# Six orders for the three products of a weight chunk, one for each loop job of each phase, and one small tensor less

## The chip, the core and the metric

The kernel runs on one core of one Trainium2 chip. The metric is the device time of one execution in microseconds (us). One execution of the kernel before was recorded by the hardware profiler; all rows below are read from it.

## The reference

Two decoder layers over 256 tokens of width 2048, all in float32. Layer 0 mixes tokens with an RWKV-7 recurrence, layer 1 with block attention over one block of keys and values; after each mixer and each FFN stands a layer norm over `ALPHA * h + branch`.

```python
mixed = _rwkv7_time_mix(h, ...)  if layer < N_A_LAYERS  else  _moba_attention(h, b_w_q[j], b_w_o[j], k_pad, v_pad, k_mean)
h = _layernorm(ALPHA * h + mixed, ln1_w[layer], ln1_b[layer])
h = _layernorm(ALPHA * h + _swiglu(h, ffn_w_gate[layer], ffn_w_up[layer], ffn_w_down[layer]),
               ln2_w[layer], ln2_b[layer])
# _swiglu: (jax.nn.silu(x @ w_gate) * (x @ w_up)) @ w_down
```

Nearly all of the arithmetic is products of the 256 tokens with weight matrices: eight of 2048x2048 (k, r, v, o, kv_k, kv_v, q and ao in the kernel's names), and for each layer gate and up (2048x5632) and down (5632x2048).

## The kernel before

A weight matrix is taken in **jobs** of 512 columns, and a job in **chunks** of 2x128 rows (KC = 2), 128x1024 numbers in SBUF. A job of 2048 rows has 8 chunks, one of the down projection 22. For each chunk SyncE loads `raw[:, s]` (512 KB), ScalarE writes the rounded high half `whi[:, s]` (line 951), VectorE writes the rest `wlo[:, s] = raw - whi` (lines 1237 and 1510), with s one of four slots (RING = 4). The activations are split too: `ahi` and `alo` (hidden ones of the FFN: `hThi` and `hTlo`).

TensorE then makes three products for a chunk, for each of its two blocks of 128 rows (k2) and each of the two halves of the tokens (t): high activations by high weights (HIHI), high by low (HILO) and low by high (LOHI). The activations are the stationary tile (128x128, loaded by an LDWEIGHTS before every matmul) and the weights are the moving tile (128x512). So a chunk has 12 matmuls. They add up in two PSUM banks, `ps[:, 2 * parity + t]`, one for each half of the tokens; parity is that of the job. In the kernel before, the order is k2, then t, then HIHI, HILO, LOHI (lines 495 to 497):

```python
pe.wait_ge(split_done, c + (ch + 1))
...
        mm(o, hi[:, k, tok], whi[:, s, k2, :], start=(k == 0), stop=False)
        mm(o, hi[:, k, tok], wlo[:, s, k2, :], start=False, stop=False)
        last = mm(o, lo[:, k, tok], whi[:, s, k2, :], start=False, stop=(k == kt - 1))
last.then_inc(chunk_used, 1)
```

The semaphore `split_done` says that both halves of a chunk are there; `chunk_used` gives the slot back to ScalarE. `job` waits for the two banks and runs its chunks. Pairs of jobs, one of each parity, stand in hardware loops: `jobs` for the projections of layer 0 (`proj`, three times one pair), the down projections (one pair of 22 chunks each), K, V and Q (`kvq`, five pairs) and the attention output (`ao`, one pair), and `ffn` for gate and up (10 pairs in each layer, with 8 transposes of the hidden tile between the jobs, line 881). The jobs before and after the loops (`first_job`, `normed_job`, `last_job`) are written out; `last_job` finishes one half of the tokens ahead of the other over its last four chunks (lines 520 to 522), so that it runs 24 matmuls into one bank.

The layer norm of a half of the tokens is VectorE's `last_block`: mean and variance, then a reciprocal square root in three Newton steps on tensors of 128x1 (lines 1544 to 1552). It uses `half_var`, a tensor of 128x2 numbers, for minus half of the variance. `small` is a tensor of 128x32 of which columns 0 and 1 are used.

Of the kernel before, what the change touches and what calls it, by code (L numbers as in the profile page):

```python
# [29 lines left out]
P = 128  # L30
D = 2048
T = 256
TT = T // P
KT = D // P
NB = 512
NJ = D // NB
FF = 5632
FT = FF // P
FB = FF // NB
KC = 2  # L40
RING = 4
PLAIN = 3
CJ = KT // KC
CF = FT // KC
LR = 96
LG = 256
HD = 64
# [47 lines left out]
PH = {}  # L95
_c = _j = 0
for _name, _jobs, _per in (("proj", 12, CJ), ("wo", NJ, CJ), ("up0", 2 * FB, CJ), ("down0", NJ, CF), ("kvq", 12, CJ),
                           ("ao", NJ, CJ), ("up1", 2 * FB, CJ), ("down1", NJ, CF)):
    assert _c % RING == 0 and _j % 2 == 0
# [30 lines left out]
def trunk(nc, x, rows, rwkv_rows, lora, w, consts, ln_rows, y):  # L130
    with ExitStack() as ctx:
# [3 lines left out]
        def sb(name, shape, dt=F32, stack=ctx):  # L135
            return stack.enter_context(nc.sbuf_tensor(name, shape, dt))
# [5 lines left out]
        whi = sb("whi", [P, RING, KC, NB], F32R)  # L142
        wlo = sb("wlo", [P, RING, KC, NB], F32R)
# [5 lines left out]
        var = sb("var", [P, TT])  # L149
        rstd = sb("rstd", [P, TT])  # L150
        small = sb("small", [P, 32])
        half_var = sb("half_var", [P, TT])
        gsm = sb("gsm", [P, 5, 8])
        nsmall = sb("nsmall", [P, 48])
        idle = sb("idle", [P, 10])
# [3 lines left out]
        ahi = sb("ahi", [P, KT, T], F32R)  # L159
        alo = sb("alo", [P, KT, T], F32R)  # L160
# [4 lines left out]
        hThi = sb("hThi", [P, FT, T], F32R)  # L165
        hTlo = sb("hTlo", [P, FT, T], F32R)
        ps = ctx.enter_context(nc.psum_tensor("ps", [P, 8, NB], F32))
# [316 lines left out]
        def _(pe):  # L484
            mm, tr = nc.tensor.matmul, nc.tensor.transpose

            def chunk(c, ch, parity, kt, hi, lo):

                s = (ch + (CF * parity if kt == FT else 0)) % RING
                pe.wait_ge(split_done, c + (ch + 1))  # L490
                for k2 in range(KC):
                    k = ch * KC + k2
                    for t in range(TT):
                        o, tok = ps[:, 2 * parity + t, :], slice(t * P, (t + 1) * P)
                        mm(o, hi[:, k, tok], whi[:, s, k2, :], start=(k == 0), stop=False)  # L495
                        mm(o, hi[:, k, tok], wlo[:, s, k2, :], start=False, stop=False)  # L496
                        last = mm(o, lo[:, k, tok], whi[:, s, k2, :], start=False, stop=(k == kt - 1))  # L497
                last.then_inc(chunk_used, 1)

            def job(c, u, parity, kt, hi, lo):  # L500

                pe.wait_ge(bank_free[parity], u + 1)
                for ch in range(kt // KC):
                    chunk(c, ch, parity, kt, hi, lo)

            def last_job(c, u, kt, hi, lo):

# [43 lines left out]
                    if src is not None and ch + 4 < CJ:  # L551
                        transposes(ch + 4)

            def jobs(c0, j0, n, kt, hi, lo):

                per = kt // KC
                with pe.Fori(0, n // 2) as i:
                    for b in range(2):
                        job(i * (2 * per) + (c0 + b * per), i + j0 // 2, b, kt, hi, lo)


            pe.wait_ge(id_in, 16)
            for g in range(KT // KC):
# [3 lines left out]
                for k2 in range(KC):  # L567
                    for t in range(TT):
                        k = g * KC + k2
                        last = tr(ps[:, 4 + g % 4, k2 * T + t * P:k2 * T + (t + 1) * P], xn[:, t, k * P:(k + 1) * P], ident[:])  # L570
# [7 lines left out]
            for n, (m, buf) in enumerate(((w1, L_), (a1, A_))):  # L578
                mx = buf.rearrange("p t (k n) -> p (t k) n", n=T)
                for k in range(KT):  # L580
                    pe.wait_ge(lmix_done, n * KT + k + 1)
                    last = mm(ps[0:LR, 4 + n, 0:T], m[:, k, :], mx[:, k, :], start=(k == 0), stop=(k == KT - 1))  # L582
# [3 lines left out]
            for k in range(KT):  # L586
                pe.wait_ge(lmix_done, 2 * KT + k + 1)
                for m in range(2):
                    last = mm(ps[:, 6 + m, 0:T], g1[:, k, m * P:(m + 1) * P], mx[:, k, :], start=(k == 0), stop=(k == KT - 1))  # L589
# [5 lines left out]
            for n in range(2 * NJ):  # L595
                if n >= 2:
                    pe.wait_ge(lora2_copied, n - 1)
                h, m = ((hw, w2), (ha, a2))[n // NJ]
                for t in range(TT):
                    last = mm(ps[:, 4 + 2 * (n % 2) + t, :], h[0:LR + 1, t * P:(t + 1) * P],  # L600
                              m[0:LR + 1, (n % NJ) * NB:(n % NJ + 1) * NB], start=True, stop=True)
                last.then_inc(lora2_made, 1)

            for n in range(3):
                c, j = n * NJ * CJ, n * NJ
                first_job(c, j // 2, act_ready, n * (KT // KC))
                job(c + CJ, j // 2, 1, KT, ahi, alo)
                jobs(c + 2 * CJ, j + 2, NJ - 2, KT, ahi, alo)
            for b in range(2):
                pe.wait_ge(bank_free[b], 7)  # L610

# [208 lines left out]
            for n in range(NJ):  # L820
                for t in range(TT):
                    for k in range(2):
                        last = mm(ps[:, 2 * n + t, :], hg[:, k, t * P:(t + 1) * P], g2[:, k, n * NB:(n + 1) * NB], start=(k == 0), stop=(k == 1))
                last.then_inc(gate_made, 1)

            c, j = PH["wo"]
# [45 lines left out]
            def ffn(layer):  # L872
                c0, j0 = PH[f"up{layer}"]
                u0 = layer * FB

                def h_transposes(i):

                    pe.wait_ge(bank_free[1], i + (j0 // 2 + 2 - u0))
                    for f in range(4):
                        for t in range(TT):  # L880
                            last = tr(ps[:, 4 + f // 2, (f % 2) * T + t * P:(f % 2) * T + (t + 1) * P], gtmp[:, t, f * P:(f + 1) * P], ident[:])  # L881
                    last.then_inc(h_tr, 1)

                normed_job(2 * layer, f"up{layer}")
                with pe.Fori(0, FB - 1) as i:
                    job(i * (2 * CJ) + (c0 + 2 * CJ), i + (j0 // 2 + 1), 0, KT, ahi, alo)
                    h_transposes(i + u0)
                    job(i * (2 * CJ) + (c0 + 3 * CJ), i + (j0 // 2 + 1), 1, KT, ahi, alo)
                    pe.wait_ge(hlo_done, i + (u0 + 1))
                h_transposes(u0 + FB - 1)  # L890
                pe.wait_ge(hlo_done, u0 + FB)
                c, j = PH[f"down{layer}"]
                jobs(c, j, NJ - 2, FT, hThi, hTlo)
                last_two(c + 2 * CF, j + 2, FT, hThi, hTlo)

            ffn(0)
            normed_job(1, "kvq")
            jobs(PH["kvq"][0] + 2 * CJ, PH["kvq"][1] + 2, 10, KT, ahi, alo)

            for b in range(2):  # L900
                pe.wait_ge(bank_free[b], PH["ao"][1] // 2 + 1)
# [1 line left out]
            with pe.Fori(0, HEADS // 4) as i:  # L903
                one = i + 1
                lane = [(al[s], 4 * s, stg[s], QKT[s], Sm[s], PT[s]) for s in range(2)]
                for q, b, st, qkt, sm, pt in lane:
                    pe.wait_ge(q["qk_staged"], one)
                    for h in range(2):
                        for n in range(4):
                            last = tr(ps[:, b + h, n * P:(n + 1) * P], st[:, n // 2, n % 2, h * P:(h + 1) * P], ident[:])  # L910
                    last.then_inc(q["qk_tr"], 1)
                for q, b, st, qkt, sm, pt in lane:
                    pe.wait_ge(q["qkt_set"], one)
                    for h in range(2):
                        mm(ps[:, b + 2 + h, 0:P], qkt[:, h, 0:P], qkt[:, h, 2 * P:3 * P], start=True, stop=True)
                        last = mm(ps[:, b + 2 + h, P:3 * P], qkt[:, h, P:2 * P], qkt[:, h, 2 * P:4 * P], start=True, stop=True)
                    last.then_inc(q["s_made"], 1)
                for q, b, st, qkt, sm, pt in lane:
                    pe.wait_ge(q["p_normed"], one)
                    for h in range(2):  # L920
                        for n in range(3):
                            last = tr(ps[:, b + h, n * P:(n + 1) * P], sm[:, h, n * P:(n + 1) * P], ident[:])
                    last.then_inc(q["pt_made"], 1)
                for q, b, st, qkt, sm, pt in lane:
                    pe.wait_ge(q["pt_set"], one)
                    pe.wait_ge(q["v_staged"], one)
                    for h in range(2):
                        v = st[:, 2, :, h * P:(h + 1) * P]
                        mm(ps[:, b + 2 + h, 0:T], v[:, 0], pt[:, h, 0:2 * P], start=True, stop=False, skip_group_check=True)
                        last = mm(ps[:, b + 2 + h, P:T], v[:, 1], pt[:, h, 2 * P:3 * P], start=False, stop=True, skip_group_check=True)  # L930
# [1 line left out]
            for q in al:  # L932
                pe.wait_ge(q["olo_set"], HEADS // 4)
            c, j = PH["ao"]
            jobs(c, j, NJ - 2, KT, ahi, alo)
            last_two(c + 2 * CJ, j + 2, KT, ahi, alo)
            ffn(1)

# [266 lines left out]
        def _(dve):  # L1205
# [37 lines left out]
            for g in range(KT // KC):  # L1243
                dve.wait_ge(xt_copied, g + 1)
                k = slice(g * KC, (g + 1) * KC)
# [247 lines left out]
            for n in range(NJ):  # L1493
                dve.wait_ge(gate_made, n + 1)
                c = slice(n * NB, (n + 1) * NB)
# [27 lines left out]
            def last_block(c0, kt, n, t):  # L1523

                c_next = c0 + NJ * kt // KC
                cs = slice((NJ - 1) * NB, NJ * NB)
                if t == 0:
                    dve.wait_ge(tile_done, n + 1)
                else:
                    dve.wait_ge(chunk_used, c_next)  # L1530
                ins = V.scalar_tensor_tensor(out=Zn[:, t, cs], in0=H[:, t, cs], scalar=ALPHA, in1=ps[:, 2 + t, :], op0=ALU.mult, op1=ALU.add)
                if t == 0 and c_next == CHUNKS:
                    then(ins)
                elif t == 0:
                    ins.then_inc(split_done, 1)
                    dve.wait_ge(split_done, c_next + 1)
                else:
                    ins.then_inc(bank_free[1], 1)
                    dve.wait_ge(bank_free[1], (c_jobs[n] + NJ - 1) // 2 + 2)
                then(V.bn_stats(stats[:, t, NJ - 1, :], Zn[:, t, cs]))  # L1540
                then(V.bn_aggr(mv[:, t, :], stats[:, t]))
                I32 = mybir.dt.int32
                x, hx, y0, q = (m[:, t:t + 1] for m in (var, half_var, rstd, small))
                ins = V.tensor_scalar(hx, mv[:, t, 1:2], LN_EPS, -0.5, ALU.add, ALU.mult)
                if c_next < CHUNKS:
                    ins.then_inc(split_done, 1)
                then(V.tensor_scalar(x, mv[:, t, 1:2], LN_EPS, None, ALU.add))
                then(V.tensor_scalar(q.bitcast(I32), x.bitcast(I32), 1, None, ALU.logical_shift_right))
                then(V.tensor_scalar(y0.bitcast(I32), q.bitcast(I32), -1.0, float(0x5F3759DF), ALU.mult, ALU.add))
                for _ in range(3):  # L1550
                    then(V.tensor_scalar(q, y0, y0, hx, ALU.mult, ALU.mult))
                    then(V.scalar_tensor_tensor(out=y0, in0=q, scalar=1.5, in1=y0, op0=ALU.add, op1=ALU.mult))
# [157 lines left out]
```

## Time and profile before

| | |
|---|---|
| median of the runs | 2715.93 us (two of three runs; the third was 13648.72 us) |
| the profiled execution | 2719.42 us, span 2717.6 us |
| TensorE busy | 2549.3 us, 94% |
| VectorE busy | 1445.9 us, 53% |
| ScalarE busy | 1084.7 us, 40% |
| mean granted clock of TensorE | 0.97 |
| matmuls, weight loads | 15342 each |
| read from HBM | 436.96 MB, 162 GB/s |

The median is the figure to compare. The span reaches from the first to the last instruction of the profiled execution; 1.8 us lie around it. A matmul's row gives the start as it was recorded and an end that is modelled, so that neighbouring rows overlap; the distance of starts is the measure of its pace.

### The profile page before, as it was taken

Reading aid. Unit: us, or ns where it says so; the run is one execution under the profiler, and the core shown is the slowest. Engines: PE = TensorE matmul, PEld = TensorE weight load, DVE = VectorE, ACT = ScalarE, POOL = GpSimd, SP = SyncE. Lnnn points to the kernel's source line nnn. Section 1 sums busy time; section 2 is a strip of 40 time slices with the busy share of each in tenths; the row PEclk is TensorE's granted clock in tenths of the full one; section 3 lists DMA queues with packets and bytes.
Section 4 is the critical chain, followed back from the end, with each engine's and each line's share of the span. In section 5 each row is a group of like instructions: output and inputs, shape, how many; then the busy total and the mean of one; then the engine's idle time right before and its main releaser. Section 6 shows DMA issues by size and latency. Waiting matters only on the chain.

```text
span 2717.6 us, 39424 instructions
## 1 busy us (share of the span) xinstructions
PE 2549.3 (94%) x15342; PEld 2042.7 (75%) x15342; DVE 1445.9 (53%) x1738; ACT 1084.7 (40%) x1326; POOL 139.3 (5%) x187
## 2 busy tenths in 40 slices
PE   7999968878999999999999999969999999999997
PEld 5777757766788888887887788857788888877886
DVE  4555976674654444444445644454754444444445
ACT  3444434433443434343333444443434343443332
POOL 1000014430000000000000000010000000000000
PEclk9999979889999999999999999989999999999999
DMA  5555700144466666665665666614566666666664
GB/s 173 166 170 168 214 21 8 15 137 149 147 199 186 180 185 184 185 179 161 186 187 183 199 190 187 185 54 147 150 196 185 182 185 184 185 179 193 186 187 131
DMA packets 219155, 440.75 MB, mean 162 GB/s; under 512 B 13216, under 2 KB 13248, under 8 KB 217824
## 3 DMA queue, kind: packets, MB, share of 16 engines
q1 hardware_dynamic: 214400, 413.19, 50.5%
q0 software_dynamic: 4640, 25.92, 3.4%
q8 instruction: 85, 1.39, 0.2%
q14 instruction: 30, 0.25, 0.0%
HBM read 436.96 MB, written 2.10 MB: 162 GB/s over the span
## 4 chain that ended last, share of the span: by engine, by line
PE 86%; DVE 9%; issue 2%; ACT 2%; DMA 1%; POOL 1%; DVEq 0%; ACTq 0%; SPq 0%; POOLq 0%
PE ps L495 25%; PE ps L496 25%; PE ps L497 25%; DVE wlo L1237 2%; PE ps L881 1%; PE ps L685 1%; PE ps L695 1%; PE ps L705 1%; PE ps L582 1%; PE ps L853 1%; DVE rec L1377 1%; DMA big<-lora_a 1%; DVE alo L1564 1%; PE ps L600 1%; PE ps L589 1%
## 5 line engine op out<-in xcount | busy, mean ns | idle before, releaser
L951 ACT CAST whi<-raw 128x1024 fp32r<-128x1024 f32 x772 | 807.6, 1049 | 1271.6 <-PE ps L497 1192.6
L1237 DVE TENSOR_TENSOR wlo<-raw,whi 128x1024 fp32r<-128x1024 f32 x551 | 672.1, 1225 | 700.5 <-ACT whi L951 700.0
L495 PE MATMUL ps<-whi,ahi 128*128 128x512 f32 x2364 | 940.7, 398 | 29.7 <-DVE wlo L1237 12.9
L496 PE MATMUL ps<-wlo,ahi 128*128 128x512 f32 x2364 | 935.5, 396 | 0.0
L497 PE MATMUL ps<-whi,alo 128*128 128x512 f32 x2364 | 935.2, 396 | 0.0
L495 PEld LDWEIGHTS ps<-whi,ahi 128*128 128x128 f32 x2364 | 444.3, 188 | 145.9 <-issue 37.0
L497 PEld LDWEIGHTS ps<-whi,alo 128*128 128x128 f32 x2364 | 444.1, 188 | 108.7
L496 PEld LDWEIGHTS ps<-wlo,ahi 128*128 128x128 f32 x2364 | 444.5, 188 | 107.2 <-issue 0.7
L1510 DVE TENSOR_TENSOR wlo<-raw,whi 128x1024 fp32r<-128x1024 f32 x224 | 274.0, 1224 | 332.7 <-ACT whi L951 332.5
L495 PE MATMUL ps<-whi,hThi 128*128 128x512 f32 x672 | 267.6, 398 | 5.1 <-DVE hTlo L1614 5.1
L496 PE MATMUL ps<-wlo,hThi 128*128 128x512 f32 x672 | 267.3, 398 | 0.0
L497 PE MATMUL ps<-whi,hTlo 128*128 128x512 f32 x672 | 267.1, 397 | 0.0
L495 PEld LDWEIGHTS ps<-whi,hThi 128*128 128x128 f32 x672 | 127.2, 189 | 37.0 <-issue 5.9
L496 PEld LDWEIGHTS ps<-wlo,hThi 128*128 128x128 f32 x672 | 127.1, 189 | 31.3
L497 PEld LDWEIGHTS ps<-whi,hTlo 128*128 128x128 f32 x672 | 127.1, 189 | 31.1
L1127 ACT ACTIVATE a2t<-ps,lnT 128x128 f32<-128x128 f32 x96 | 34.2, 496 | 34.1 <-PE ps L843 34.1
L1377 DVE TENSOR_TENSOR rec<-ps,big 128x512 f32<-128x512 f32 x40 | 27.6, 690 | 35.4 <-PE ps L685 34.8
L450 POOL DMA_DIRECT2D big<-ln_rows x3 | 1.7, 572 | 871.6 <-PE ps L522 851.1
L1251 DVE SCALAR_TENSOR_TENSOR big<-big,mixT 128x256 f32<-128x256 f32 x96 | 40.0, 479 | 1.5 <-PE ps L582 0.8
L1383 DVE STREAM_TRANSPOSE rec<-ps 128x512 f32<-128x512 f32 x32 | 22.8, 713 | 32.7 <-PE ps L695 32.4
L1614 DVE TENSOR_TENSOR hTlo<-ps,hThi 128x1024 f32 (+1 forms) x22 | 26.9, 1224 | 21.1 <-ACT hThi L1146 21.1
L695 PE MATMUL ps<-big,rec 64*64 64x64 f32 x960 | 32.2, 233 | 4.1 <-DVE rec L1377 3.9
(286 smaller groups left out, 1681.7 us busy)
## 6 DMA issues: line engine op xcount, KB each, us to landing
raw<-w_gate SPq DMA_DIRECT2D x176, 512.0 KB, 3.7
raw<-w_up SPq DMA_DIRECT2D x176, 512.0 KB, 3.7
raw<-w_down SPq DMA_DIRECT2D x176, 512.0 KB, 3.7
raw<-w_k SPq DMA_DIRECT2D x32, 512.0 KB, 4.2
raw<-w_r SPq DMA_DIRECT2D x32, 512.0 KB, 3.7
raw<-w_v SPq DMA_DIRECT2D x32, 512.0 KB, 4.4
raw<-w_o SPq DMA_DIRECT2D x32, 512.0 KB, 4.3
raw<-kv_k SPq DMA_DIRECT2D x32, 512.0 KB, 4.2
```

The costliest lines, as they stand in the source:

```text
L495: mm(o, hi[:, k, tok], whi[:, s, k2, :], start=(k == 0), stop=False)
L496: mm(o, hi[:, k, tok], wlo[:, s, k2, :], start=False, stop=False)
L497: last = mm(o, lo[:, k, tok], whi[:, s, k2, :], start=False, stop=(k == kt - 1))
L582: last = mm(ps[0:LR, 4 + n, 0:T], m[:, k, :], mx[:, k, :], start=(k == 0), stop=(k == KT - 1))
L589: last = mm(ps[:, 6 + m, 0:T], g1[:, k, m * P:(m + 1) * P], mx[:, k, :], start=(k == 0), stop=(k == KT - 1))
L695: quarters(lambda j, h, t, a, u, v: mm(ps[u, 2 + a, half(j)], Z[v, a, half(j)], XS[v, half(j)] if a else XT[g % 2][v, 0, half(j)], start=T ...
L951: nc.scalar.copy(whi[:, s], raw[:, s]).then_inc(hi_done, 1)
L1127: ins = A(hF[:, k, t * P:(t + 1) * P], ps[:, 4 + b, k2 * P:(k2 + 1) * P], ACT.Identity, scale=lnT[:, (n * 2) * KT + k:(n * 2) * KT + k + 1 ...
L1237: V.tensor_tensor(wlo[:, s], raw[:, s], whi[:, s].bitcast(F32), ALU.subtract).then_inc(split_done, 1)
L1251: return V.scalar_tensor_tensor(out=out, in0=xxT[:, k], scalar=mixT[:, m * KT + k:m * KT + k + 1], in1=xT[:, k, 1:T + 1], op0=ALU.mult, op ...
L1377: V.tensor_tensor(Z.rearrange("p l (j c) -> p l j c", c=CHUNK), ps[:, 0:2, 0:4 * CHUNK].rearrange("p l (j c) -> p l j c", c=CHUNK), mask_l ...
L1510: V.tensor_tensor(wlo[:, s], raw[:, s], whi[:, s].bitcast(F32), ALU.subtract).then_inc(split_done, 1)
```

## The change

A table of six orders is added, and `chunk` walks through one of them. The flags `start` and `stop` go to the first and the last matmul of each token half in the job. The matmuls, their weight loads, the wait at the chunk's first and the semaphore at its last instruction are as many as before. The loops name an order for each of their two jobs: (1, 3), (2, 4) and (5, 0) for the three projections, (2, 4) and (5, 1) for the FFN of layers 0 and 1, (1, 3) and (4, 5) for their down projections, (1, 3) for K, V and Q and (3, 0) for the attention output. All jobs outside of the loops keep order 0, which is the old one. `half_var` is gone; columns 2 and 3 of `small` take its place, and the tensors that were allocated behind it start 32 bytes lower in SBUF (`ahi` from 67936 to 67904).

```diff
+HIHI, HILO, LOHI = range(3)
+ORDERS = (
+    [(k2, t, p) for k2 in range(KC) for t in range(TT) for p in (HIHI, HILO, LOHI)],
+    [(k2, t, p) for k2 in range(KC) for p in (HIHI, HILO, LOHI) for t in range(TT)],
+    [(k2, t, p) for k2 in range(KC) for t in range(TT) for p in (HILO, HIHI, LOHI)],
+    [(k2, t, p) for k2 in range(KC) for t, p in ((0, HIHI), (0, LOHI), (1, HIHI), (1, LOHI), (0, HILO), (1, HILO))],
+    [(k2, t, p) for p in (HIHI, HILO, LOHI) for t in range(TT) for k2 in range(KC)],
+    [(k2, t, p) for k2 in range(KC) for t in range(TT) for p in (HIHI, LOHI, HILO)],
+)
...
-        half_var = sb("half_var", [P, TT])
...
-            def chunk(c, ch, parity, kt, hi, lo):
+            def chunk(c, ch, parity, kt, hi, lo, order=0):
...
                 pe.wait_ge(split_done, c + (ch + 1))
-                for k2 in range(KC):
+                for at, (k2, t, p) in enumerate(ORDERS[order]):
                     k = ch * KC + k2
...
+                    a, m = ((hi, whi), (hi, wlo), (lo, whi))[p]
+                    first = ch == 0 and t not in [x[1] for x in ORDERS[order][:at]]
+                    final = ch == kt // KC - 1 and t not in [x[1] for x in ORDERS[order][at + 1:]]
+                    last = mm(ps[:, 2 * parity + t, :], a[:, k, t * P:(t + 1) * P], m[:, s, k2, :], start=first, stop=final)
                 last.then_inc(chunk_used, 1)
...
-                jobs(c + 2 * CJ, j + 2, NJ - 2, KT, ahi, alo)
+                jobs(c + 2 * CJ, j + 2, NJ - 2, KT, ahi, alo, ((1, 3), (2, 4), (5, 0))[n])
...
-                    job(i * (2 * CJ) + (c0 + 2 * CJ), i + (j0 // 2 + 1), 0, KT, ahi, alo)
+                    job(i * (2 * CJ) + (c0 + 2 * CJ), i + (j0 // 2 + 1), 0, KT, ahi, alo, (2, 5)[layer])
                     h_transposes(i + u0)
-                    job(i * (2 * CJ) + (c0 + 3 * CJ), i + (j0 // 2 + 1), 1, KT, ahi, alo)
+                    job(i * (2 * CJ) + (c0 + 3 * CJ), i + (j0 // 2 + 1), 1, KT, ahi, alo, (4, 1)[layer])
...
-                x, hx, y0, q = (m[:, t:t + 1] for m in (var, half_var, rstd, small))
+                x, hx, y0, q = (m[:, t:t + 1] for m in (var, small[:, TT:2 * TT], rstd, small))
```

TensorE, in the FFN loop of layer 0, where the second job begins after the transposes. Before (names are out<-moving,stationary):

```order
L881 MATMUL ps<-ident,common 128x128 x8
L490 REGISTER_ALU
L495 MATMUL ps<-whi,ahi 128x512
L496 MATMUL ps<-wlo,ahi 128x512
L497 MATMUL ps<-whi,alo 128x512
L495 MATMUL ps<-whi,ahi 128x512
```

and with the change, in which this job has order 4:

```order
L888 MATMUL ps<-ident,common 128x128 x8
L498 REGISTER_ALU
L504 MATMUL ps<-whi,ahi 128x512 x4
L504 MATMUL ps<-wlo,ahi 128x512 x4
L504 MATMUL ps<-whi,alo 128x512 x4
```

The 12 matmuls of the chunk stand in three groups of four instead of four groups of three. In the first job of the same loop, order 2, the rows of a chunk read with the change:

```order
L498 ISA
L504 MATMUL ps<-wlo,ahi 128x512
L504 MATMUL ps<-whi,ahi 128x512
L504 MATMUL ps<-whi,alo 128x512
L504 MATMUL ps<-wlo,ahi 128x512
```

The product with the low half stands first, and after the two with the high half comes the next token half. On VectorE the rows of a token half's layer norm (after `last_block`'s sum) were

```order
L1541 BN_AGGR mv<-stats 128x2
L1544 TENSOR_SCALAR half_var<-mv 128x1
L1547 TENSOR_SCALAR var<-mv 128x1
L1548 TENSOR_SCALAR small<-var 128x1
L1549 TENSOR_SCALAR rstd<-small 128x1
L1551 TENSOR_SCALAR small<-rstd,half_var 128x1
```

and with the change

```order
L1548 BN_AGGR mv<-stats 128x2
L1551 TENSOR_SCALAR small<-mv 128x1
L1554 TENSOR_SCALAR var<-mv 128x1
L1555 TENSOR_SCALAR small<-var 128x1
L1556 TENSOR_SCALAR rstd<-small 128x1
L1558 TENSOR_SCALAR small<-rstd,small 128x1
```

Nothing has moved there; one operand's tensor is another.

## Rows read from the trace of the kernel before

**Rows 1.** The page: span and busy time by engine

```profile
span 2717.6 us, 39424 instructions
...
PE 2549.3 (94%) x15342; PEld 2042.7 (75%) x15342; DVE 1445.9 (53%) x1738; ACT 1084.7 (40%) x1326; POOL 139.3 (5%) x187
```

**Rows 2.** The page: the chain that ended last, shares of the span by line

```profile
PE ps L495 25%; PE ps L496 25%; PE ps L497 25%; DVE wlo L1237 2%; PE ps L881 1%; PE ps L685 1%; PE ps L695 1%; PE ps L705 1%; PE ps L582 1%; PE ps L853 1%; DVE rec L1377 1%; DMA big<-lora_a 1%; DVE alo L1564 1%; PE ps L600 1%; PE ps L589 1%
```

**Rows 3.** Timeline of TensorE: start us, duration us, engine, line, op

```profile
703.27 0.40 PE L495 MATMUL ps<-whi,ahi 128*128 128x512 f32 x1
703.51 0.39 PE L496 MATMUL ps<-wlo,ahi 128*128 128x512 f32 x1
703.74 0.40 PE L497 MATMUL ps<-whi,alo 128*128 128x512 f32 x1
...
704.44 0.39 PE L497 MATMUL ps<-whi,alo 128*128 128x512 f32 x1
704.67 0.40 PE L495 MATMUL ps<-whi,ahi 128*128 128x512 f32 x1
...
708.87 0.40 PE L495 MATMUL ps<-whi,ahi 128*128 128x512 f32 x1
...
709.58 0.39 PE L520 MATMUL ps<-whi,ahi 128*128 128x512 f32 x1
...
715.17 0.39 PE L520 MATMUL ps<-whi,ahi 128*128 128x512 f32 x1
```

**Rows 4.** Windows: stretch, length, busy us of each engine, clock, DMA share

```profile
800.00:1200.00 400.00, 400.00 (x1750) 322.36 (x1749) 192.84 (x159) 162.41 (x158) 0.00 (x0) 1.00 0.64 184
1200.00:1300.00 100.00, 93.92 (x397) 75.17 (x396) 41.88 (x35) 36.15 (x35) 0.00 (x0) 0.95 0.55 165
```

**Rows 5.** Timeline of all engines inside the FFN loop of layer 0

```profile
1199.10 1.23 DVE L1237 TENSOR_TENSOR wlo<-raw,whi 128x1024 fp32r<-128x1024 f32 x1 [1.57 <-ACT whi L951]
...
1200.62 0.40 PE L495 MATMUL ps<-whi,ahi 128*128 128x512 f32 x1
1200.62 0.19 PEld L496 LDWEIGHTS ps<-wlo,ahi 128*128 128x128 f32 x1
1200.82 1.05 ACT L951 CAST whi<-raw 128x1024 fp32r<-128x1024 f32 x1 [1.75 <-PE ps L497]
1200.85 0.39 PE L496 MATMUL ps<-wlo,ahi 128*128 128x512 f32 x1
```

**Rows 6.** Waits of TensorE: who waited for whom, us in total, times, longest

```profile
PE ps L495 <- DVE wlo L1237: 12.9, 13, 3.0
```

**Rows 7.** Groups of weight loads by line: count, busy us, mean ns

```profile
L496 PEld LDWEIGHTS ps<-wlo,ahi 128*128 128x128 f32 x2364 | 444.5, 188 | 107.2 <-issue 0.7
...
L497 PEld LDWEIGHTS ps<-whi,alo 128*128 128x128 f32 x2364 | 444.1, 188 | 108.7
```

**Rows 8.** Operations on small tensors: count, duration ns min/median/max

```profile
L1551 DVE TENSOR_SCALAR small<-rstd,half_var x24: 272/273/275, 717.7 to 2708.5; 128x1 f32<-128x1 f32 x24
L1544 DVE TENSOR_SCALAR half_var<-mv x8: 153/154/156, 717.1 to 2706.8; 128x1 f32<-128x1 f32 x8
...
L1552 DVE SCALAR_TENSOR_TENSOR rstd<-small,rstd x24: 158/159/161, 718.1 to 2708.8; 128x1 f32<-128x1 f32 x24
...
L1549 DVE TENSOR_SCALAR rstd<-small x8: 153/153/154, 717.6 to 2707.3; 128x1 int32<-128x1 int32 x8
```

**Rows 9.** Lines 644 and 1251: count, duration ns min/median/max, starts

```profile
L644 PEld LDWEIGHTS ps<-ident,rec x24: 140/230/230, 373.1 to 528.7; 128*128 128x128 f32 x24
L644 PEld LDWEIGHTS ps<-ident,a2t x24: 139/143/230, 395.5 to 555.7; 128*128 128x128 f32 x24
...
L1251 DVE SCALAR_TENSOR_TENSOR big<-big,mixT x96: 469/479/487, 17.9 to 267.8; 128x256 f32<-128x256 f32 x96
```

**Rows 10.** Timeline of TensorE after the pause at 159 us

```profile
164.05 0.77 PE L495 MATMUL ps<-whi,ahi 128*128 128x512 f32 x1 [4.63 <-issue]
...
165.04 0.63 PE L497 MATMUL ps<-whi,alo 128*128 128x512 f32 x1
165.47 0.63 PE L495 MATMUL ps<-whi,ahi 128*128 128x512 f32 x1
```

More of the change, by code:

```diff
@@ L485, in _, with job @@
             mm, tr = nc.tensor.matmul, nc.tensor.transpose
-            def chunk(c, ch, parity, kt, hi, lo):
+            def chunk(c, ch, parity, kt, hi, lo, order=0):
                 s = (ch + (CF * parity if kt == FT else 0)) % RING
                 pe.wait_ge(split_done, c + (ch + 1))
-                for k2 in range(KC):
+                for at, (k2, t, p) in enumerate(ORDERS[order]):
                     k = ch * KC + k2
[L493 to L497, printed above, removed]
+                    a, m = ((hi, whi), (hi, wlo), (lo, whi))[p]
+                    first = ch == 0 and t not in [x[1] for x in ORDERS[order][:at]]
+                    final = ch == kt // KC - 1 and t not in [x[1] for x in ORDERS[order][at + 1:]]
+                    last = mm(ps[:, 2 * parity + t, :], a[:, k, t * P:(t + 1) * P], m[:, s, k2, :], start=first, stop=final)
                 last.then_inc(chunk_used, 1)
-            def job(c, u, parity, kt, hi, lo):
+            def job(c, u, parity, kt, hi, lo, order=0):
                 pe.wait_ge(bank_free[parity], u + 1)
                 for ch in range(kt // KC):
-                    chunk(c, ch, parity, kt, hi, lo)
+                    chunk(c, ch, parity, kt, hi, lo, order)
             def last_job(c, u, kt, hi, lo):
@@ L552, in first_job, with jobs @@
                         transposes(ch + 4)
-            def jobs(c0, j0, n, kt, hi, lo):
+            def jobs(c0, j0, n, kt, hi, lo, orders):
                 per = kt // KC
@@ L558, in jobs @@
                     for b in range(2):
-                        job(i * (2 * per) + (c0 + b * per), i + j0 // 2, b, kt, hi, lo)
+                        job(i * (2 * per) + (c0 + b * per), i + j0 // 2, b, kt, hi, lo, orders[b])
             pe.wait_ge(id_in, 16)
@@ L892, in ffn @@
                 c, j = PH[f"down{layer}"]
-                jobs(c, j, NJ - 2, FT, hThi, hTlo)
+                jobs(c, j, NJ - 2, FT, hThi, hTlo, ((1, 3), (4, 5))[layer])
                 last_two(c + 2 * CF, j + 2, FT, hThi, hTlo)
@@ L897, in _ @@
             normed_job(1, "kvq")
-            jobs(PH["kvq"][0] + 2 * CJ, PH["kvq"][1] + 2, 10, KT, ahi, alo)
+            jobs(PH["kvq"][0] + 2 * CJ, PH["kvq"][1] + 2, 10, KT, ahi, alo, (1, 3))
             for b in range(2):
@@ L934, in _ @@
             c, j = PH["ao"]
-            jobs(c, j, NJ - 2, KT, ahi, alo)
+            jobs(c, j, NJ - 2, KT, ahi, alo, (3, 0))
             last_two(c + 2 * CJ, j + 2, KT, ahi, alo)
```

## The prediction

> **What bounds the kernel now.** I first read the head of the page. TensorE is busy for 2549.3 of 2717.6 us, VectorE for 53% and ScalarE for 40% of the span [rows 1]. Of the chain that ended last, three quarters are the lines 495 to 497 on TensorE, the three products of a weight chunk; the largest share of another engine is 2% [rows 2]. TensorE is therefore the bound. What matters for an edit that only reorders those three lines is the pitch: the time from the start of one matmul to the start of the next. A row's own duration of 396 ns overlaps its neighbour and says nothing of it.
>
> The timeline of TensorE gives the pitch. Eight groups of three, 24 matmuls, start from 703.27 to 708.87 us: 5.60 us, so 233.3 ns each [rows 3]. A chunk has 12 of them, 2.80 us. In a stretch of 400 us inside a loop TensorE has no idle time and the granted clock is 1.00 [rows 4]. 512 columns at 2.4 GHz, which is what a granted clock of 1.00 stands for, are 213.3 ns, so 20.0 ns of each pitch are something else.
>
> Supply is not the limit. ScalarE makes the high half of a chunk in 1.05 us and then stands for 1.75 us until TensorE gives a slot back; VectorE makes the low half in 1.23 us and stands for 1.57 us [rows 5]. The chain of a refill is 1.05 + 1.23 us plus hand-over, under 2.5 us, from the end of chunk n to the readiness of chunk n+4, which is wanted three chunks or 8.4 us later. In the whole run TensorE waits at line 495 for a low half only 12.9 us in 13 places [rows 6].
>
> **The change, part by part.** The loops named in the diff run 552 chunks: 48 in the three projections, 160 in each FFN, 44 in each down projection, 80 for K, V and Q and 16 for the attention output. Order 0 keeps 16 of them (the second job of the third projection and of the attention output). So 536 chunks, 6432 matmuls, are reordered; at 233.3 ns they are 1500.8 us, 55% of the span. By orders: 150 chunks run order 1, 88 order 2, 78 order 3, 110 order 4, 110 order 5.
>
> What is not changed: a chunk still has 12 matmuls with 12 weight loads; its first instruction still waits for the low half of the whole chunk, and its last still hands the slot back. So no wait moves relative to the chunk, even where an order begins with the low half (order 2), and nothing is queued behind a new wait. All six orders begin with a stationary tile of the high activations, as before. Per engine the instruction counts are equal, so the loops' code is as long as before.
>
> What is changed is the neighbourhood of each matmul. Each transition can keep or change the PSUM bank, the stationary tile and the moving tile. I counted them over the 552 chunks, chunk borders included.
>
> (a) Bank changes: 4 a chunk before; 12, 4, 8, 6 and 4 in orders 1 to 5. In sum 2208 before, 3940 after, 1732 more. The trace has both kinds: from 709.58 us the last job runs 24 matmuls into one bank, and its 24th start after that is 715.17 us: 5.59 us, against 5.60 us for the 24 in which 8 change the bank [rows 3]. Two readings to 0.01 us can be off by 0.02 us together, over 8 changes 2.5 ns each. I take zero; the bound is 1732 x 2.5 ns = 4.3 us either way.
>
> (b) Repeated stationary tiles: 4 a chunk before (line 495 to 496), kept only by orders 0 and 2; 2208 before, 416 after, 1792 fewer. If a repeated tile were cheaper, 495 to 496 would be the short step. It is 0.24 us at one place, where the next one is 0.23 [rows 3], and 0.23 us at another [rows 5]. The load of line 496, which repeats the tile, takes a mean of 188 ns over the run, as that of 497 does [rows 7]. The repeat is loaded again and costs the same. I take zero; with 5 ns of reading error the bound is 1792 x 5 = 9.0 us either way.
>
> (c) One neighbourhood is new: same bank, new stationary tile, same moving tile (high-high, then low-high for the same tokens). Orders 2, 3 and 5 have 4 a chunk: 276 x 4 = 1104. No row of before shows it. Its two nearest rows differ in one thing each: 496 to 497 (same bank, both tiles new) is 0.23 us, 497 to 495 from one token half to the other (new bank, same moving tile; 704.44 to 704.67 us) 0.23 us [rows 3]. I take the same 233.3 ns. Downward it can't go below the columns: -20.0 ns x 1104 = -22.1 us. Upward the far bound is a weight load that comes out from under the running matmul, which is a rival below.
>
> (d) The half-variance moves into columns 2 and 3 of another small tensor. Two operations use it: 24 of 273 ns at line 1551 read it, 8 of 154 ns at line 1544 write it [rows 8]. These stand on the path between the last product and the next phase. After the change line 1551 reads and writes one tensor, at different columns. The nearest row is line 1549, which reads that small tensor and takes 153 ns, where line 1544, which reads and writes elsewhere, takes 154 [rows 8]. I take zero. If 1551 fell to line 1552's 159 ns it would give 24 x 0.114 = 2.7 us; if all 32 doubled they would cost 24 x 0.273 + 8 x 0.154 = 7.8 us.
>
> (e) The tensors behind it start 32 bytes lower, among them both activation halves. Weight loads of 128x128 from rec, ahead of it, and from a2t, behind it, show minima of 140 and 139 ns [rows 9], though their starts differ by 32 bytes modulo 64. VectorE's line 1251 reads rows that start 4 bytes further each time and stays within 469 to 487 ns over 96 runs [rows 9]. Zero.
>
> The sum: 2719.42 us of the profiled execution (span 2717.6 and 1.8 around it) + 0 = 2719.4 us. That execution is 3.5 us or 0.13% over the median of the runs, 2715.93 us, so the forecast is the median, **2716 us**.
>
> **Rivals.** First, slower: in the new neighbourhood (c) the weight load is no longer taken ahead. Now a load starts with the matmul before the one that it serves, as at 1200.62 us, and is done after 0.19 us, 0.04 us before it is wanted [rows 5]. If the moving tile held back the load in these 1104 places, each would show up to 187 ns: 206 us, 2922 us. It decides (2%, 54.3 us) from 49 ns per place, or 290 fully exposed loads. Against it: the step 497 to 495 keeps the moving tile too, and hides its load [rows 3].
>
> Second, faster: the 20.0 ns over the columns are a price of the old order, for instance of three products in a row into one bank, and all reordered matmuls lose it: 6432 x 20.0 ns = 128.6 us, 2587 us. The supply could follow: the chunk would be 2.56 us against 1.23 us of VectorE work. Against it: the pitch is the same within one bank and over changes of it. The Trainium skill (TensorE: Matmul & The Clock Gate, "Wait — 56ns, not 53.3ns?") measured 215.7 ns for 512 columns with bf16, 17.6 ns under the 233.3 ns here; by that figure the same rival would be an estimated 113 us, 2603 us. The trace does not agree with the figure at any transition.
>
> Third, the phase of the clock. After a pause of 4.63 us, at 159 us, the next starts are 0.43 us apart, the 1.2 GHz level, where they are 0.23 us apart otherwise [rows 3, 10]. The 100 us from 1200 us have such a stretch too and a mean clock of 0.95 [rows 4]: 5% of full speed missing over 100 us is 5 us lost. None of the pauses is touched, but one more such stretch would cost about that, one less would give it back. That stays inside "no change".
>
> That the change does nothing at all is the forecast itself; that it is not carried out is excluded by the rows of the order.
>
> **How the numbers follow.** No change to speak of: 0.94. Load exposed: 0.03, ends slower. The 20 ns lost: 0.03, ends faster. The low end takes (c) down to its floor, 2716 - 22 = 2694 us. The high end takes (a) and (b) at their bounds, 2716 + 13.3 = 2729, with a little of the clock 2730 us. Between them lies more than 8 in 10; I don't narrow it, since these are the bounds of what no row excludes. Faster or slower by over 2%, which is about what a measurement of this kernel can tell, has 0.03 each, within 2% 0.94.
>
> **What would show it.** In the changed kernel's timeline the 12 starts of a chunk in orders 1 to 5 must span 2.80 us; a load after "high-high, low-high" must still start with the matmul before; the window from 800 to 1200 us must be 400 us busy at 1.00 with as many matmuls; line 1551's successor must stay at 273 ns. Wrong would be: steps of unequal length within a chunk, a weight load that begins after its neighbour's start, or idle time at the chunk's first matmul.

## The result and the profile after

The changed kernel takes 2681.2 us (median of four runs, 2677.46 to 2682.99), the kernel before 2715.93 us. The ratio of the runs is 0.9871, with a 95% interval of 0.9852 to 0.989. It is faster by 34.7 us, 1.3%. The forecast was 2716 us with a range of 2694 to 2730 us; the result lies 13 us under its low end.

The page of the changed kernel: span and busy time, chain by line, and the groups of the products (as in [rows 1], [rows 2] and [rows 7]; all six lines of products now have line 504):

```profile
span 2681.0 us, 39424 instructions
...
PE 2513.0 (94%) x15342; PEld 2047.2 (76%) x15342; DVE 1446.8 (54%) x1738; ACT 1086.0 (41%) x1326; POOL 138.8 (5%) x187
...
PE ps L504 74%; DVE wlo L1244 2%; PE ps L888 1%; PE ps L702 1%; PE ps L692 1%; PE ps L712 1%; PE ps L589 1%; PE ps L860 1%; DVE big L1258 1%; DVE rec L1384 1%; PE ps L607 1%; PE ps L596 1%; DVE alo L1571 1%; PE ps L529 0%; PE ps L527 0%
...
L504 PEld LDWEIGHTS ps<-whi,ahi 128*128 128x128 f32 x2364 | 445.3, 189 | 131.9 <-issue 36.7
L504 PEld LDWEIGHTS ps<-whi,alo 128*128 128x128 f32 x2364 | 446.6, 189 | 101.9
L504 PEld LDWEIGHTS ps<-wlo,ahi 128*128 128x128 f32 x2364 | 446.9, 189 | 98.9 <-issue 0.7
```

The instruction counts are the same, and the busy times of the other engines are within 1.3 us of what they were. TensorE's fell by 36.3 us, where the span lost 36.6 us. The waits of TensorE at these products did not fall. Before, they were 12.9 us for the low half [rows 6], and

```profile
PE ps L495 <- issue: 11.6, 3, 4.6
```

With the change they are

```profile
PE ps L504 <- DVE wlo L1244: 13.1, 14, 3.1
PE ps L504 <- issue: 11.6, 3, 4.6
```

So the products themselves came closer together. The windows of the changed kernel (as [rows 4]; the number in brackets behind TensorE's busy time counts its matmuls):

```profile
800.00:1200.00 400.00, 400.00 (x1786) 329.32 (x1785) 195.91 (x161) 166.95 (x161) 0.00 (x0) 1.00 0.64 188
```

At the same granted clock of 1.00 the 400 us hold 1786 matmuls, where they held 1750 [rows 4].

The telling rows are those of a place that the orders don't touch. The last job of the first output projection is written out and keeps the old order. The timeline of TensorE there, the first row and the one 24 matmuls later (before: 709.58 to 715.17 us, 5.59 us [rows 3]):

```profile
703.66 0.39 PE L527 MATMUL ps<-whi,ahi 128*128 128x512 f32 x1
...
709.16 0.39 PE L527 MATMUL ps<-whi,ahi 128*128 128x512 f32 x1
```

That is 5.50 us, 229 ns a matmul. And the two jobs that are written out ahead of the first loop, and so ahead of every reordered chunk, already have that pitch. Twelve steps of the old order in the second of them:

```profile
100.06 0.39 PE L504 MATMUL ps<-whi,ahi 128*128 128x512 f32 x1
100.29 0.39 PE L504 MATMUL ps<-wlo,ahi 128*128 128x512 f32 x1
100.52 0.39 PE L504 MATMUL ps<-whi,alo 128*128 128x512 f32 x1
...
102.80 0.40 PE L504 MATMUL ps<-whi,ahi 128*128 128x512 f32 x1
```

2.74 us, 228 to 229 ns. Meanwhile two stretches show the old pitch of 233.3 ns: the second projection of layer 0 (161.8 to 252.8 us) and K, V and Q (1496 to 1748 us), both with jobs of the old order and reordered ones in them. In the loop for K, V and Q, from the first to the second of these rows there are 24 matmuls of order 3, 5.60 us:

```profile
1600.05 0.40 PE L504 MATMUL ps<-whi,ahi 128*128 128x512 f32 x1
...
1605.65 0.40 PE L504 MATMUL ps<-whi,ahi 128*128 128x512 f32 x1
```

I took all the records of starts and cut them into groups of 12 products that follow one another without another matmul between them. Of 724 groups, 119 are at 233.3 ns and most of the others (570) at 228.9. All the products of this kind are 3 x (2364 + 672) in the loops' lines and 192 in the last jobs, 9300. (1 - 119/724) x 9300 x 4.44 ns = 34.5 us, which accounts for the gain of 34.7 us. All six orders occur at 228.9 ns, and orders 0 to 4 at 233.3 ns too. The cause was thus to be looked for in the other half of the edit: without the half-variance tensor the activation halves start at 67904, not 67936.

### The profile page after: what moved, and what is told of

It reads as the page before. It is cut to its first block, busy times and chain, and to the rows that moved or that the text cites. A ratio compares the mean times of both kernels' runs of the same rounds, so it can differ in the third digit from the quotient of the medians.

```text
span 2681.0 us, 39424 instructions
## 1 busy us (share of the span) xinstructions
PE 2513.0 (94%) x15342; PEld 2047.2 (76%) x15342; DVE 1446.8 (54%) x1738; ACT 1086.0 (41%) x1326; POOL 138.8 (5%) x187
## 4 chain that ended last, share of the span: by engine, by line
PE 85%; DVE 10%; ACT 2%; issue 2%; DMA 1%; POOL 1%; DVEq 0%; ACTq 0%; POOLq 0%
PE ps L504 74%; DVE wlo L1244 2%; PE ps L888 1%; PE ps L702 1%; PE ps L692 1%; PE ps L712 1%; PE ps L589 1%; PE ps L860 1%; DVE big L1258 1%; DVE rec L1384 1%; PE ps L607 1%; PE ps L596 1%; DVE alo L1571 1%; PE ps L529 0%; PE ps L527 0%
## 5 line engine op out<-in xcount | busy, mean ns | idle before, releaser
L504 PE MATMUL ps<-whi,ahi 128*128 128x512 f32 x2364 | 853.0, 397 | 29.7 <-DVE wlo L1244 13.1
L504 PE MATMUL ps<-whi,alo 128*128 128x512 f32 x2364 | 845.5, 393 | 0.0
L504 PE MATMUL ps<-wlo,ahi 128*128 128x512 f32 x2364 | 828.8, 394 | 0.0
L504 PE MATMUL ps<-whi,hThi 128*128 128x512 f32 x672 | 247.3, 395 | 5.1 <-DVE hTlo L1621 5.1
L504 PE MATMUL ps<-whi,hTlo 128*128 128x512 f32 x672 | 247.1, 395 | 0.0
L504 PE MATMUL ps<-wlo,hThi 128*128 128x512 f32 x672 | 239.4, 394 | 0.0
```

What stands on the lines that cost most here:

```text
L504: last = mm(ps[:, 2 * parity + t, :], a[:, k, t * P:(t + 1) * P], m[:, s, k2, :], start=first, stop=final)
```

## Experiments

Each kernel below is one of the two kernels of the case with a small edit. Theory A: the starts of the tiles in SBUF set the pitch. Theory B: the orders do. The weight halves stand ahead of the half-variance tensor in the list of tensors, at 32896, and did not move.

**The slot alone.** The kernel before, with this edit only:

```diff
-        half_var = sb("half_var", [P, TT])
...
-                x, hx, y0, q = (m[:, t:t + 1] for m in (var, half_var, rstd, small))
+                x, hx, y0, q = (m[:, t:t + 1] for m in (var, small[:, TT:2 * TT], rstd, small))
```

> The old order in every job; only the half-variance tensor is gone, so that the activation halves start 32 bytes lower (67904 in place of 67936). Theory A (the start of the activation tiles modulo 64 bytes sets the pitch): the whole gain is here, 2675 to 2685 us, pitch 228.9 ns in most stretches. Theory B (the orders bring it): 2716 us, pitch 233.3 ns everywhere.

2681.76 us, ratio 0.9857 (0.984 to 0.9874): the whole gain. This edit also changes the operand on VectorE; that it is not the cause is seen in the kernels below, where a spare tensor alone moves the pitch.

**The orders alone.** The changed kernel, with the tensor put back:

```diff
+        half_var = sb("half_var", [P, TT])
...
-                x, hx, y0, q = (m[:, t:t + 1] for m in (var, small[:, TT:2 * TT], rstd, small))
+                x, hx, y0, q = (m[:, t:t + 1] for m in (var, half_var, rstd, small))
```

> The six orders, with the half-variance tensor kept, so that every tensor starts where it did before. Theory A: 2716 us and 233.3 ns in all orders. Theory B: 2675 to 2685 us.

2716.78 us, ratio 1.0001 (0.9991 to 1.0011). The window of this kernel:

```profile
800.00:1200.00 400.00, 400.00 (x1750) 322.36 (x1749) 192.53 (x158) 162.07 (x157) 0.00 (x0) 1.00 0.63 184
```

The 400 us hold 1750 matmuls as before. Theory B has fallen: six orders, 6432 reordered matmuls, and nothing to measure.

**32 bytes higher.** The kernel before, with a spare tensor ahead of the activations, which start at 67968:

```diff
         idle = sb("idle", [P, 10])
+        spare = sb("spare", [P, 8])
```

> The old order and the half-variance tensor kept; a spare tensor of 32 bytes is put ahead of the activations, which start at 67968, a multiple of 64 and of 128. Theory A with a grain of 64 bytes: as with 32 bytes less, 2675 to 2685 us. With a grain of 128 (67904 is 64 past a multiple of 128): another time, 2716 us or something between. Theory B: 2716 us.

2653.8 us, ratio 0.9757 (0.974 to 0.9774), better than both kernels of the case. That was outside of what either theory had foreseen. The timeline of its last job, 24 matmuls apart, and its window:

```profile
701.27 0.39 PE L521 MATMUL ps<-whi,ahi 128*128 128x512 f32 x1
...
706.71 0.39 PE L521 MATMUL ps<-whi,ahi 128*128 128x512 f32 x1
```

```profile
800.00:1200.00 400.00, 400.00 (x1803) 331.93 (x1802) 197.67 (x162) 168.59 (x163) 0.00 (x0) 1.00 0.65 189
```

5.44 us, 226.7 ns, and that is the pitch in every stretch. 9300 x 6.6 ns = 61 us, nearly all of the 63 us by which it is under the kernel before (2716.92 us on the same chip).

**The weights moved instead.** The same 32 bytes ahead of both operands, so that the weights start at 32928 and the activations at 67968:

```diff
+        spare = sb("spare", [P, 8])
         with ExitStack() as early:
             rec2 = sb("rec2", [P, 8192], stack=early)
```

> The old order; the spare 32 bytes stand ahead of the weight halves, so that the moving tiles start 32 bytes past a multiple of 64 and the stationary tiles at one. If only the stationary tile's start matters: 2675 to 2685 us. If each of the two must start at a multiple of 64, or if they must start alike modulo 64: 2716 us, pitch 233.3 ns. Theory B: 2716 us.

2715.48 us, ratio 0.9994 (0.9984 to 1.0004). The activations start where they did in the kernel with 32 bytes more, but the pace is the old one. So it is not the stationary tile's start alone that counts. The distance of the two starts is 35040 here and in the kernel before. That gave theory R: only the distance counts, modulo some grain. Its rival, theory O: each operand pays for its own start.

**Both at 32.** Weights at 32928, activations at 68000: neither is a multiple of 64, and the distance is that of the kernel with 32 bytes more.

```diff
+        spare = sb("spare", [P, 8])
         with ExitStack() as early:
             rec2 = sb("rec2", [P, 8192], stack=early)
...
         idle = sb("idle", [P, 10])
+        spare2 = sb("spare2", [P, 8])
```

> The old order; spare tensors put the weight halves at 32928 and the activation halves at 68000, both 32 past a multiple of 128. Theory R (only the distance of the two operands' starts modulo 128 counts; so far 0 gave 226.7 ns, 64 mostly 228.9 and 96 233.3): distance 0, 226.7 ns, 2650 to 2660 us. Theory O (each operand must start at a multiple of 64, or pays for itself): 233.3 ns or more, 2716 us or more.

2657.13 us, ratio 0.9781 (0.9764 to 0.9797). The timeline of the last job, 24 apart:

```profile
697.56 0.39 PE L522 MATMUL ps<-whi,ahi 128*128 128x512 f32 x1
...
703.00 0.39 PE L522 MATMUL ps<-whi,ahi 128*128 128x512 f32 x1
```

5.44 us again. Theory O has fallen; the distance counts.

**The activations at 32** past a multiple of 128, the weights unmoved (a spare tensor of 16 numbers in place of 8, ahead of the activations).

> The old order; weight halves at 32896 (multiple of 128), activation halves at 68000 (32 past one). Theory R: distance 32, not measured before; equal to 96 if the sign does not count, 233.3 ns and 2716 us. Theory O: 233.3 ns, as with 96, since it is 32 past a multiple of 64.

2716.97 us in one run, 5.60 us for the 24 (707.28 to 712.88): 233.3 ns. Both theories had that, so this run tells them apart no further; it gives the pitch at distance 32.

**The weights at 64** (a spare tensor of 16 numbers ahead of the weights, and the half-variance tensor dropped).

> The old order without the half-variance tensor; weight halves at 32960 (64 past a multiple of 128), activation halves at 67968 (a multiple of 128). Theory R: distance 64, 228.9 ns in most stretches, about 2680 us. Theory O with a grain of 128 for the stationary tile alone: 226.7 ns, 2654 us.

2679.68 us in one run, 5.49 us for the 24 (703.47 to 708.96): as in the changed kernel, at other starts and the same distance, and as theory R had it; the 2654 us of the rival did not come. The stretches at 233.3 ns are not the same, though: here the second projection, most of the third (285.7 to 331.8 us) and the first gate and up jobs of layer 1 (1932 to 1983 us) are at 233.3 ns, while K, V and Q run at 228.9. In the kernel with the slot alone it is K, V and Q and those first jobs of layer 1.

**The low half of the weights alone** moved by 32 bytes; the high half and the activations start as in the kernel with 32 bytes more:

```diff
         whi = sb("whi", [P, RING, KC, NB], F32R)
+        spare = sb("spare", [P, 8])
         wlo = sb("wlo", [P, RING, KC, NB], F32R)
```

> The old order; as in the kernel with 32 bytes more (226.7 ns), but the low weight half starts 32 past a multiple of 128 while the high half stays at one. If the price is paid matmul by matmul: only the steps that begin or end at the product with the low half are longer, a mean near 229 ns, 2675 to 2685 us. If one misplaced tensor slows the whole stream: 233.3 ns, 2716 us. Theory O with the stationary tile alone: 226.7 ns.

2701.86 us in one run, between the two cases foreseen. The timeline of the down projection, three steps of a kind and the row 12 matmuls on:

```profile
1300.41 0.39 PE L496 MATMUL ps<-whi,hThi 128*128 128x512 f32 x1
1300.64 0.40 PE L497 MATMUL ps<-wlo,hThi 128*128 128x512 f32 x1
1300.88 0.39 PE L498 MATMUL ps<-whi,hTlo 128*128 128x512 f32 x1
1301.10 0.39 PE L496 MATMUL ps<-whi,hThi 128*128 128x512 f32 x1
...
1303.18 0.39 PE L496 MATMUL ps<-whi,hThi 128*128 128x512 f32 x1
```

2.77 us for 12, 231 ns. In this down projection the three steps have means of 230.8 ns (from line 496), 236.7 (from line 497, the low half's product) and 225.8 (from line 498): against 226.7 ns, the two steps that end or begin at the misplaced tile are 4.1 and 10.0 ns longer, and the third is 0.9 ns shorter. K, V and Q look the same. But in the gate and up loops, 3840 of the 9300 products, the same layout runs at the old pace. The row at the start of a group of three and the one 12 matmuls on:

```profile
1000.35 0.40 PE L496 MATMUL ps<-whi,ahi 128*128 128x512 f32 x1
...
1003.15 0.40 PE L496 MATMUL ps<-whi,ahi 128*128 128x512 f32 x1
```

2.80 us, 233.3 ns, though two of the three products have the best distance, and the window from 800 to 1200 us holds 1751 matmuls, where the kernel before has 1750. In the groups of 12 of the whole run 336 are at 233.3 ns, 223 at 231.1 and 134 at 231.7. So neither of the two cases foreseen holds alone: the price is partly paid at the misplaced product, and in other stretches it holds the whole stream at 233.3 ns. What decides between them is open.

**A wider grain.** Activations at 68096: the distance is 35200, a multiple of 128 but not of 256 (spare of 40 numbers).

> The old order; activation halves at 68096, weight halves at 32896: the distance is a multiple of 128 but, unlike in the kernel with 32 bytes more, not of 256. Theory R128 (nothing beyond 128 counts): 226.7 ns, 2650 to 2660 us. Theory R256 (the distance modulo 256 counts): a longer pitch than 226.7 ns, towards 228.9.

2704.93 us, ratio 0.9953 (0.9935 to 0.9972). The timeline of the last job, 24 apart:

```profile
708.43 0.39 PE L521 MATMUL ps<-whi,ahi 128*128 128x512 f32 x1
...
714.00 0.39 PE L521 MATMUL ps<-whi,ahi 128*128 128x512 f32 x1
```

5.57 us, 232 ns: a grain of 128 is too narrow. The pitch is longer than 226.7 ns, as theory R256 had it, but not near the 228.9 ns that it leant to.

Activations at 68224: the distance is a multiple of 512 (spare of 72 numbers).

> The old order; activation halves at 68224, so that the distance is a multiple of 512, the bytes of one stationary tile's row. Theory R128: 226.7 ns, 2650 to 2660 us. If the price goes on halving with a wider grain: under 226.7 ns, 2620 to 2640 us.

2657.38 us, ratio 0.979 (0.9773 to 0.9806), 5.44 us for the 24 (696.00 to 701.44): the same 226.7 ns as at a multiple of 256 only. The grain is 256.

**The orders where the distance is right** (spare of 16 numbers in the changed kernel, activations at 67968).

> The six orders, with activation halves at 67968 (distance a multiple of 128). The orders bring nothing by this theory: 226.7 ns in all of them, 2650 to 2660 us, as the old order at the same starts (2653.8). If orders count where the starts are right: a difference to it of over 5 us.

2658.52 us, ratio 0.9793 (0.9777 to 0.9809), 5.44 us for the 24 (699.35 to 704.79). The interval of the old order at these starts, 0.974 to 0.9774, ends just below, a gap of under 0.1%, and the 4.7 us between the two medians are inside the 5 us that the expectation allowed; the pitch is 226.7 ns with both, and the kernel with a distance of a multiple of 512, in the old order, has 2657.38 us. The orders bring nothing here either.

**Distance 96**, a spare of 32 numbers.

> The old order; activation halves at 68064, 96 past a multiple of 256 from the weight halves (32896). If the size of the distance alone counts, falling away from 32: between the 233.3 ns at 32 and the 232.4 ns at 128, 2700 to 2718 us. If an odd multiple of 32 is always the worst: 233.3 ns, 2716 us.

2726.4 us in one run. The timeline of its last job, 24 matmuls apart:

```profile
713.09 0.40 PE L521 MATMUL ps<-whi,ahi 128*128 128x512 f32 x1
...
718.72 0.40 PE L521 MATMUL ps<-whi,ahi 128*128 128x512 f32 x1
```

5.63 us, and 1747 matmuls in the window from 800 to 1200 us: the slowest of all, slower than both expectations had it.

**Distance 64**, a spare of 24 numbers.

> The old order; activation halves at 68032, 64 past a multiple of 256 from the weight halves; 192 was 228.9 ns in most stretches. If the sign of the distance does not count: 228.9 ns, 2675 to 2685 us. If it does: another pitch.

2718.77 us in one run. The window of this kernel:

```profile
800.00:1200.00 400.00, 400.00 (x1750) 321.97 (x1749) 192.76 (x158) 161.89 (x157) 0.00 (x0) 1.00 0.63 184
```

1750 matmuls as before, and 5.60 us for the 24 (708.39 to 713.99). 64 is not like 192, so the sign counts there; 32 and 224 have the same pitch.

The whole series, where "distance" is the start of the activation halves less that of the weight halves, modulo 256 (it is the same for every slot, tile and hidden half). The labels are e1 for the slot alone, e2 for the orders alone, and so on: e3 32 bytes higher, e4 the weights moved, e5 both at 32, e6 the activations at 32, e7 the wider grain, e8 the weights at 64, e10 the multiple of 512, e11 the orders at the right distance, e12 distance 96, e13 distance 64. The kernel before took 2716.9 to 2717.5 us in the rounds of these runs; e6, e8, e12 and e13 are single runs. The low half alone (e9) is left out, since its two weight halves have different distances, 0 and 224.

| distance | kernel | starts (weights, activations) | 24 matmuls of the last job | time |
|---|---|---|---|---|
| 0 | e3, e5, e10, e11 | 32896, 67968; 32928, 68000; 32896, 68224; 32896, 67968 | 5.44 us each | 2653.8, 2657.1, 2657.4, 2658.5 us |
| 32 | e6 | 32896, 68000 | 5.60 us | 2717.0 us |
| 64 | e13 | 32896, 68032 | 5.60 us | 2718.8 us |
| 96 | e12 | 32896, 68064 | 5.63 us | 2726.4 us |
| 128 | e7 | 32896, 68096 | 5.57 us | 2704.9 us |
| 192 | changed, e1, e8 | 32896, 67904 (twice); 32960, 67968 | 5.50, 5.49, 5.49 us | 2681.2, 2681.8, 2679.7 us |
| 224 | before, e2, e4 | 32896, 67936 (twice); 32928, 67968 | 5.59, 5.60, 5.60 us | 2715.9, 2716.8, 2715.5 us |

160 was not run. Nor was any distance that is no multiple of 32.

## Why the prediction was wrong

**What bounds the kernel, and how its pace is read**, was right: the gain is in the pitch of the products and nowhere else.

**(a), (b), (c), the three neighbourhoods**, were right at zero: with the old starts the six orders have a ratio of 1.0001, and with the best starts the pitch is 226.7 ns in both. No stretch of the changed kernel ties its pitch to an order. The new neighbourhood, "high-high, low-high", costs what the others do.

**(d), the operand in another tensor**, was right. The row of the changed kernel:

```profile
L1558 DVE TENSOR_SCALAR small<-rstd,small x24: 272/273/276, 711.7 to 2671.8; 128x1 f32<-128x1 f32 x24
```

**(e), the 32 bytes, is the step that failed.** It was put at zero and got no bound at all; measured, it is 35 us in this change and 63 us in the other direction. The evidence was of the wrong kind. The durations of weight loads do not show it: those of the products are 189 ns in the changed kernel against 188 [rows 7], the longer in the faster kernel. The loads of line 644 were not alike to begin with: only their minima, 140 and 139 ns, were compared, and the medians in the same rows are 230 and 143 ns [rows 9]. VectorE's line 1251 says nothing of TensorE. What changed was the time from the start of one matmul to that of the next, and all products of the kernel before had one and the same distance of tiles (224 modulo 256). So the equal pitch of all its transitions, on which I had built, could not tell what else it depended on. A term that moves both operands of the bound engine against each other, and that no row varies, should have had the whole 20.0 ns over the columns as its bound: 9300 x 20.0 ns = 186 us down.

The range missed with it: its low end, 2694 us, came from (c) alone, which gave nothing. That the time stayed within 2%, to which the prediction gave 0.94, was luck: 34.7 us happen to be under 54.3 us, and no term of the sum had sized them. At distance 0, 64 bytes further up, the same kernel with the same orders is 2.1% under the kernel before.

**The rivals.** "A load that comes out from under the matmul" did not occur. The second had the right place and the wrong owner: a third of the 20.0 ns over the columns can be had (6.6 ns), by starts and not by orders. The figure of the Trainium skill (TensorE: Matmul & The Clock Gate, "Wait — 56ns, not 53.3ns?"), 215.7 ns, was reached in no run; the lowest is 226.7 ns. The section names no number type for it, and the matmuls that its page begins with are bf16; those here are float32r.

The third, the clock, stayed as it was: 0.97 in both profiles.

## What to carry to other kernels

Where a stream of weight loads and matmuls bounds a kernel, its pace per matmul against the columns' time is worth a look, and so are the starts of the stationary and the moving tensors in SBUF. For float32r tiles of 128x128 and 128x512, rows of 512 and 2048 bytes, a distance that is a multiple of 256 bytes gave the shortest pitch of those tried, in all three pairs of starts. And an edit that drops or adds a small tensor moves all behind it: compare it with a kernel that keeps the slot before its time is put down to the rest of the edit.

## What the runs showed of the hardware

- The pitch of a float32r matmul of 512 columns with its own weight load was 226.7 ns at a distance of 0 modulo 256, 228.9 at 192 in most stretches, 232.4 at 128, 233.3 at 32, 64 and 224, and 234.3 at 96 (means over the groups of 12 of a run, but for 192, where the two paces stand apart; 232.4 is the mean of steps of 228 to 241 ns). Why the distance counts, and whether the two reads share anything, no run shows. The Trainium skill (TensorE: Matmul & The Clock Gate, "Step-by-step: what each phase is for") says that "Loading the next tile's weights doesn't steal SBUF read bandwidth from the running matmul." Taken alone, that would lead one to expect no effect of the distance; the trace shows one of 6.6 ns in 233.3, and the measurement decides.
- At distance 192 the same code ran at either of two paces, 228.9 and 233.3 ns, each constant over tens of microseconds. K, V and Q are slow in the changed kernel and in e1, not in e8; the second projection is slow in the changed kernel and in e8, not in e1. The pace need not change at a pause of TensorE: in e8 it went from 233.3 to 228.9 ns at 331.83 us, where a single step was 0.31 us long. What chooses stays open; at distance 0 one pace alone was seen.
- With the high weight half at distance 0 and the low half at 224 (e9), the stream ran at 231.1, 231.7 or 233.3 ns, according to the stretch.
- All runs of the sweep are with the granted clock at 1.00 in the window from 800 to 1200 us.
